# Attention of eight sampled queries rearranged inside a hybrid decoder layer, with the first layer norm applied later

## The chip, the cores and the metric

The kernel runs on one core of one Trainium2 chip. The metric is the device time of one execution in microseconds; lower is better. Engines are named as in the profile: PE (TensorE), PEld (its weight loads), DVE (VectorE), ACT (ScalarE), POOL (GpSimd) and SP (SyncE, which here only issues transfers).

## The reference

One decoder layer is applied to 1024 prompt positions and to 8 sampled tokens, each with 2048 cached positions. Cut to what matters here:

```python
def sparse_attend(q, ks, vs, valid):            # 8 heads of 64; 256 selected keys per query
    logits = einsum('bthd,btkhd->bthk', q, ks) * HEAD_DIM ** -0.5
    p = softmax(where(valid, logits, NEG_INF))
    return einsum('bthk,btkhd->bthd', p, vs)

def sample_attention(...):                      # per sampled token: indexer scores over 2048 + 1 keys
    _, idx = lax.top_k(sc, 256)
    ks = where(idx < past, cache_k[page, offset], k_new)      # rows of 512 floats, gathered
    vs = where(idx < past, cache_v[page, offset], v_new)
    return sparse_attend(q, ks, vs, valid)

def merge_and_channel_mix(x, attn, gm, ga, gb, ...):
    h = layer_norm(ALPHA * x + (ga * (attn @ w_a) + gb * (gm @ w_b)) @ w_o, ln1_g, ln1_b)
    f = hierarchical_moe(h, ...)                # top group of 4, then top 2 of its 8 experts
    return layer_norm(ALPHA * h + f, ln2_g, ln2_b)
```

The prompt attends in the same way over its own 1024 keys; there the kernel masks the keys that were not chosen instead of gathering the chosen ones.

## The kernel before

The program is a row of blocks. All engines leave a block together, and each engine runs its own instruction list in order; semaphores order the engines among themselves.

1. `project_and_score` makes q, k, v and the indexer scores.
2. `choose_keys_and_gate` finds the 256 best keys on DVE while PE makes the gates `gate_a` and `merged_b` (L787), which SP stores to DRAM (L710). At its end `keep["rows"]` holds the cache row numbers of the sampled queries.
3. `attend` is written out as 34 steps over `units`: 8 query tiles t = 7 down to 0, four head pairs each. In step s, PE makes the logits of unit s (L1173), transposes the probabilities of unit s-1 (`turn_probs`, L1187), and weighs the values for unit s-2 (`weigh`, L1200). DVE adds the masks and takes the minimum (L1385) and copies part of the transposed probabilities (L1296); ACT does the exponentials (L1312) and the other copies. After the last pair of a tile PE spreads the reciprocals of the sums (L1213), ACT copies them (L1323), and DVE scales the output (`share_out`, L1372). Tiles 7 to 4 have more than 512 keys and are called wide here, tiles 3 to 0 narrow. The eight sampled queries ride along: POOL issues their 48 indirect gathers (16 of cached K rows, 16 of cached V rows, 8 and 8 of own rows), each step's behind a chunk copy of that step (`wait_for_turn`). In steps 18 to 25, PE spreads query b over all 128 partitions (`spread_query`, L1222), and DVE multiplies and reduces both halves of its K rows (L1345, L1347). The maximum, exponential, normalisation, transposition and weighting of the sampled logits follow in steps 26 to 30; copying, turning and reading the sampled output (L1326, L1258, L1411) come after the loop.
4. `merge_route_and_experts` multiplies by `w_a` (L1639), merges with the gates, multiplies by `w_o` (L1668) for 9 token tiles, adds the residual (L1905), transposes, routes (`pick`), ranks (`place`) and scatters each token's place in a list to DRAM (L1607). DVE applies the first layer norm in two passes over a tile, subtract-and-gain (L1935) and scale-and-bias (L1943). SP stores the normalised tiles to `scratch["h"]` (L1590). POOL then gathers the tokens of the first packs from it (L1983). A pack is 128 rows; 24 packs pass through the class `Experts`: transpose rows (L2113), gate and up (L2100), transpose hidden (L2121), down (L2132), scatter (L2078). Copies L2145 (ACT) and L2184 (DVE) bring the transposed rows to SBUF. The first pack is put together on PE (`assemble_first`, L1730 and L1737). Expert weights come in with 2 MB (`w_gate_up`) and 1 MB (`w_down`) loads, four experts ahead. `Finish` makes the output with the second layer norm.

Of the kernel before, what the change touches and what calls it, by code (L numbers as in the profile page):

```python
# [20 lines left out]
P = 128  # L21
D = 1024
# [46 lines left out]
def project_and_score(nc, ins, outs, keep):  # L69
# [5 lines left out]
    with nc.cleanup_on_exit(), ExitStack() as ctx:  # L75
# [91 lines left out]
        def _(sp):  # L167
# [25 lines left out]
            sp.dma_start(outs["v_all"][SEQ:, :], zs[3 * FEW:3 * FEW + N_SAMPLE, :]).then_inc(few_out, 16)  # L193
            for t in range(NT):
# [20 lines left out]
            sp.wait_ge(few_out, 48)  # L215
# [172 lines left out]
        def _(act):  # L388
# [11 lines left out]
            def read(t, g):  # L400
                bank = FIRST_BANKS[g] if t == 0 else g % 2
                act.wait_ge(acc_full, 1 + 4 * t + g + 1)
                if g == 0 and t == 1:
                    act.wait_ge(few_out, 48)
                    act.wait_ge(turned_full, 1)
# [185 lines left out]

def choose_keys_and_gate(nc, ins, outs, keep, scratch):


    with nc.cleanup_on_exit(), ExitStack() as ctx:
# [85 lines left out]
        idle = [sem(f"idle{n}") for n in range(3)]  # L681

# [42 lines left out]
        def _(pe):  # L725
# [92 lines left out]
            make_gates(KC // 2 - 1, ahead=find_rows)  # L818

# [125 lines left out]
        def _(dve):  # L945
# [85 lines left out]
            step(nc.vector.tensor_copy(keep["rows"][:], rows_f[:]))  # L1031


def attend(nc, ins, outs, keep, scratch):
# [3 lines left out]
    PAIRS = HEADS // 2  # L1038
    n_qh = N_SAMPLE * HEADS
    with nc.cleanup_on_exit(), ExitStack() as ctx:  # L1040
# [9 lines left out]
        k_half = [keep["w_a"][:].rearrange("p a (b n) -> p (a b) n", n=AW), sb("k_sel", [P, N_SAMPLE, AW])[:]]  # L1050
        v_sel = sb("v_sel", [P, 2 * N_SAMPLE, AW])
        first = sb("first_masks", [P, 3 * P])
        probs = [sb(f"probs{j}", [P, 2, SEQ]) for j in range(2)]
# [7 lines left out]
        own_row = sb("own_row", [2, N_SAMPLE], U32)  # L1061
        lg = sb("lg", [P, 2, n_qh])
# [7 lines left out]
        k_in, v_in = sem("k_sel_in"), sem("v_sel_in")  # L1070
# [12 lines left out]
        q_spread = sem("q_spread")  # L1083
# [10 lines left out]
        query_at = {narrow + 2 + b: b for b in range(N_SAMPLE)}  # L1094
        MAX_AT, EXP_AT, PROBS_AT, TURN_AT, WEIGH_AT = (max(query_at) + n for n in (1, 2, 3, 4, 5))
# [4 lines left out]
        copies = [by[:i + 1].count(by[i]) for i in range(len(chunks))]  # L1100

# [18 lines left out]
        @block.sync  # L1120
        def _(sp):
            wait_for_gates_stored(sp)
            sp.dma_start(first[:], ins["first_masks"]).then_inc(const_in, 16)
            sp.dma_start(own_b[:], ins["rank"][:, 0:N_SAMPLE]).then_inc(own_in, 16)
            sp.wait_ge(lg_ready, N_SAMPLE // 2)
            sp.dma_start(keep["w_a"][:], ins["w_a"]).then_inc(w_a_in, 16)
            sp.wait_ge(w_a_in, 16)

        @block.gpsimd
        def _(pool):  # L1130
# [11 lines left out]
            def wait_for_turn(n):  # L1142
                wait_copied(pool, chunk_of[n, 1, units[n][0] // 4 * 4])

            for b in range(N_SAMPLE):
                wait_for_turn(b)
                for half in range(2):
                    gather(k_of, "cache_k", b, half, k_in)
            pool.wait_ge(own_ready, 1)
            pool.wait_ge(k_in, 32 * N_SAMPLE)  # L1150
            for b in range(N_SAMPLE):
                wait_for_turn(N_SAMPLE + b)
                gather_own(k_of, "k_all", b, k_in)
                gather(v_of, "cache_v", b, 0, v_in)
            pool.wait_ge(v_in, 16 * N_SAMPLE)
            for b in range(N_SAMPLE):
                wait_for_turn(2 * N_SAMPLE + b)
                gather(v_of, "cache_v", b, 1, v_in)
                gather_own(v_of, "v_all", b, v_in)
            pool.wait_ge(k_in, 48 * N_SAMPLE)  # L1160
            pool.wait_ge(v_in, 48 * N_SAMPLE)

        @block.tensor
        def _(pe):
            def make_logits(n):
                t, hp = units[n]
                if n >= 1:
                    pe.wait_ge(masked, 2 * n)
                width = (t + 1) * P
                for c in range(0, width, 512):  # L1170
                    c1 = min(width, c + 512)
                    for e in range(2):
                        mm = nc.tensor.matmul(ps[:, 2 * e + c // 512, 0:c1 - c],  # L1173
# [44 lines left out]
            def spread_query(b):  # L1218
                if b >= 2:
                    pe.wait_ge(lg_ready, b - 1)  # L1220
                for k in range(AW // P):
                    mm = nc.tensor.matmul(ps[:, 1 + 2 * (b % 2), k * P:(k + 1) * P],  # L1222
                                          qT[:, k, SEQ + b:SEQ + b + 1].to_broadcast([P, P]), ident[:],
                                          start=True, stop=True)
                mm.then_inc(q_spread, 1)

# [13 lines left out]
            def weigh_sample():  # L1240
                pe.wait_ge(pT_ready, 1)
                pe.wait_ge(v_in, 48 * N_SAMPLE)
# [9 lines left out]
            def turn_sample_out():  # L1252
                wait_copied(pe, len(chunks) - 2)
                wait_copied(pe, len(chunks) - 1)
                for g in range(2):
                    pe.wait_ge(s_copied, g + 1)
                    for k in range(AW // P):
                        mm = nc.tensor.transpose(ps[:, TURN + g, k * P:(k + 1) * P], product[g][:, k * P:(k + 1) * P], ident[:])  # L1258
                    mm.then_inc(s_turned, 1)

            for s in range(LAST):
                if s < N:
                    make_logits(s)
                if s in query_at:
                    spread_query(query_at[s])
# [4 lines left out]
                if s == WEIGH_AT:  # L1270
                    weigh_sample()
                if 0 <= s - 1 < N:
# [7 lines left out]
            turn_sample_out()  # L1280
# [19 lines left out]
        def _(act):  # L1300
            for s in range(LAST):
# [12 lines left out]
                if s == EXP_AT:  # L1314
                    act.wait_ge(lg_ready, N_SAMPLE + 2)
                    nc.scalar.activation(prob_s[:], ps[0:n_qh, 1, 0:TOPK], ACT.Exp, bias=stat_s[:, 1:2],
                                         scale=SCALE, accum_out=stat_s[:, 2:3]).then_inc(s_exped, 1)
                if s >= 2 and units[s - 2][1] == PAIRS - 1:
# [5 lines left out]
            for g in range(2):  # L1324
                act.wait_ge(s_out, g + 1)
                nc.scalar.copy(product[g][:], ps[:, 1 + 2 * g, :]).then_inc(s_copied, 1)  # L1326

        @block.vector
        def _(dve):
            step = Chain(dve, dve_step)  # L1330

            wait_for_gates_stored(dve)
# [1287 lines left out]
```

## Time and profile before

| | us |
|---|---|
| median of 3 runs | 1386.04 |
| lowest and highest | 1384.17, 1386.59 |
| the profiled execution, its own time | 1384.73 |
| its span, first to last instruction | 1383.1 |
| PE busy | 1320.8 (95%) |
| DVE busy | 717.7 (52%) |
| ACT busy | 280.1 (20%) |
| POOL busy | 241.0 (17%) |
| mean granted TensorE clock | 0.986 |

The profiled execution took 1.6 us more than its span. A matmul with fp32 operands appears as two entries, so counts of matmuls and weight loads are twice those in the source. Matmuls are pipelined: one entry's duration is longer than the distance to the next start, so in a dense stretch the distances are what counts. "Idle before" names what an engine waited for.

### The profile page before, as it was taken

The page shows a single profiled execution, that of the slowest core. Times are in us where ns is not written, and L with a number is a line of the kernel's source. Part 1 is how long each engine was busy: PE and PEld are TensorE (multiplying, and loading weights), DVE is VectorE, ACT ScalarE, POOL GpSimd, SP SyncE. Part 2 cuts the span into 40 slices and gives each one's busy share as a digit, 9 for nine tenths or more (in the row PEclk, how much of TensorE's full clock was granted, in tenths as well). Part 3 has the DMA queues.
Part 4 walks back from the last instruction along what each step waited for, and adds up shares of the span by engine and source line. Part 5 has one row for each costly group of instructions (what it writes and reads, how often), then busy time and mean ns, then how long its engine had stood idle before and what let it go on. Part 6 is the DMA issues. An engine that isn't in the chain of part 4 may idle for free. (4 is left out here: it accounts for less than half of the span.)

```text
span 1383.1 us, 19214 instructions
## 1 busy us (share of the span) xinstructions
PE 1320.8 (95%) x6689; PEld 679.1 (49%) x6689; DVE 717.7 (52%) x1709; ACT 280.1 (20%) x621; POOL 241.0 (17%) x292
## 2 busy tenths in 40 slices
PE   8999999899999999999899989999978999999994
PEld 2444444345466666666577656544443333333321
DVE  0211123589888988997265864588871111111135
ACT  0100112322221111111356430000001111111124
POOL 3222000043420000011133410011112111111113
PEclk9999999999999999999999999999999999999997
DMA  9311002210031111110032309831137999999936
GB/s 325 102 52 63 17 17 77 92 52 1 0 110 69 69 68 69 68 68 32 29 99 68 120 25 355 343 153 35 42 107 271 369 414 401 409 411 413 381 156 242
DMA packets 70316, 214.13 MB, mean 155 GB/s; under 512 B 16059, under 2 KB 41915, under 8 KB 59866
## 3 DMA queue, kind: packets, MB, share of 16 engines
q1 hardware_dynamic: 52810, 180.51, 34.7%
q0 software_dynamic: 12688, 27.76, 5.9%
q10 hardware_dynamic: 4736, 4.75, 1.1%
q8 instruction: 52, 0.85, 0.3%
q14 instruction: 30, 0.25, 0.1%
HBM read 186.47 MB, written 34.65 MB: 160 GB/s over the span
## 5 line engine op out<-in xcount | busy, mean ns | idle before, releaser
L262 PE MATMUL ps_mixer<-front,x_all 128*128 128x512 f32 (+1 forms) x448 | 180.4, 557 | 1.7 <-ACT wi L413 1.7
L959 DVE TENSOR_SCALAR_CACHE_REDUCE front<-score,bound 128x384 bf16<-128x384 f32 (+2 forms) x198 | 174.0, 940 | 0.4 <-DVE bound L981 0.3
L262 PEld LDWEIGHTS ps_mixer<-front,x_all 128*128 128x128 f32 x448 | 83.2, 190 | 91.7 <-issue 78.7
L1668 PE MATMUL ps<-w_o,mergedT 128*128 128x512 f32 x256 | 116.5, 601 | 0.0
L2100 PE MATMUL ps<-w_gate_up,w_o 128*32 128x512 f32 (+1 forms) x640 | 113.2, 594 | 1.7 <-DVE w_o L2184 1.7
L787 PE MATMUL ps_mixer<-x_all,front 128*128 128x344 f32 x384 | 114.4, 453 | 0.0
L787 PE MATMUL ps_mixer<-x_all,w_gate 128*128 128x344 f32 x384 | 113.3, 453 | 0.0
L2100 PE MATMUL ps<-w_a,w_o 128*64 128x512 f32 (+1 forms) x256 | 113.1, 595 | 0.0
L2209 DVE TENSOR_TENSOR w_o<-w_o,ps 128x256 f32<-128x256 f32 x24 | 10.1, 421 | 164.0 <-ACT w_o L2164 164.0
L787 PEld LDWEIGHTS ps_mixer<-x_all,w_gate 128*128 128x128 f32 x384 | 72.7, 190 | 37.5
L787 PEld LDWEIGHTS ps_mixer<-x_all,front 128*128 128x128 f32 x384 | 72.6, 190 | 37.1
L959 DVE TENSOR_SCALAR_CACHE_REDUCE front<-score_s,bound 8x2049 bf16<-8x2049 f32 x33 | 77.0, 2335 | 0.0
L1668 PEld LDWEIGHTS ps<-w_o,mergedT 128*128 128x128 f32 x256 | 46.0, 190 | 47.8 <-issue 47.8
L941 POOL TENSOR_TENSOR front<-front 128x344 f32<-128x344 f32 x24 | 25.2, 1050 | 243.7 <-ACT front L901 243.7
L2100 PEld LDWEIGHTS ps<-w_gate_up,w_o 128*32 128x32 f32 (+1 forms) x640 | 33.1, 115 | 69.0 <-issue 69.0
L2078 POOL DMA_INDIRECT pair_out<-w_o,entries x24 | 25.0, 1042 | 234.7 <-DVE w_o L2216 234.7
L898 ACT ACTIVATE front<-ps_mixer,gate_bias 128x344 f32<-128x344 f32 x48 | 26.2, 547 | 175.8 <-PE ps_mixer L787 175.7
L2132 PE MATMUL ps<-w_down,w_o 128*32 128x512 f32 (+1 forms) x320 | 59.3, 610 | 0.0
L2132 PE MATMUL ps<-gates,w_o 128*32 128x512 f32 (+1 forms) x128 | 58.1, 597 | 0.5 <-ACT w_o L2169 0.5
L735 PE MATMUL ps_mixer<-front,x_all 128*128 128x512 f32 x128 | 57.4, 592 | 0.0
L2100 PE MATMUL ps<-mergedT,w_o 128*32 128x512 f32 x384 | 56.5, 594 | 0.0
L1639 PE MATMUL ps<-attnT,w_a 128*128 128x344 f32 x186 | 54.0, 453 | 1.5 <-PEq L1040 1.5
(349 smaller groups left out, 1891.1 us busy)
## 6 DMA issues: line engine op xcount, KB each, us to landing
w_gate_up<-in_w_gate_up SPq DMA_DIRECT2D x16, 2048.0 KB, 14.4
w_down<-in_w_down SPq DMA_DIRECT2D x16, 1024.0 KB, 16.0
w_a<-in_w_gate_up SPq DMA_DIRECT2D x8, 2048.0 KB
mergedT<-in_w_gate_up SPq DMA_DIRECT2D x8, 2048.0 KB
gates<-in_w_down SPq DMA_DIRECT2D x8, 1024.0 KB, 7.1
mergedT<-in_w_down SPq DMA_DIRECT2D x8, 1024.0 KB
front<-in_w_qkvi SPq DMA_DIRECT2D x7, 930.0 KB, 18.0
w_gate<-in_w_gate SPq DMA_DIRECT2D x4, 1280.0 KB, 6.3
```

The costliest lines, as they stand in the source:

```text
L262: mm = nc.tensor.matmul(ps[:, g % 2, 0:c1 - c0], x_all[:, k, t * P:(t + 1) * P], w[:, k, c0:c1], start=(k == 0), stop=(k == KC - 1))
L735: mm = nc.tensor.matmul(ps[:, bank, :], x_all[:, k, t * P:(t + 1) * P], w_uv(k)[:, half * GW:(half + 1) * GW], start=(k == 0), stop=(k == ...
L787: mm = nc.tensor.matmul(ps[:, SETS[at % 2][which], 0:n], w_gate[j][:, which * KC + k, :], right[:, k, c0:c0 + n], start=(k == 0), stop=(k ...
L898: op = nc.scalar.activation(to, src, ACT.Sigmoid, bias=gate_bias[:, which, bass.ds(i * 2 + j, 1)])
L941: nc.gpsimd.tensor_tensor(m[:, 1, 0:n], m[:, 1, 0:n], m[:, 2, 0:n], ALU.mult).then_inc(multiplied, 1)
L959: V.tensor_scalar(waste[0:n, at - width:at], s, column(bound, g), None, compare, ALU.add, accum_out=column(number, g)).then_inc(taken, 1)
L1639: mm = nc.tensor.matmul(ps[:, FIRST_BANK + n % 3, 0:width], w_a[:, k, blk * P:(blk + 1) * P], attnT[:, k, c0:c0 + width], start=(k == 0), ...
L1668: mm = nc.tensor.matmul(ps[:, PROJECTED[i % 2][c], :], mergedT[:, k, t * P:(t + 1) * P], w_o[:, k, c * 512:(c + 1) * 512], start=(k == 0), ...
L2078: pool.indirect_dma_start(out=scratch["pair_out"].rearrange("t w q j d -> (t w q j) d"), out_offset=bass.IndirectOffsetOnAxis(ap=entries[: ...
L2100: mm = nc.tensor.matmul(ps[c0:c1, GU, :], rowsT[j][:, k, c0:c1], w_gu[b][:, k, :], start=(k == 0), stop=(k == KC - 1))
L2132: mm = nc.tensor.matmul(ps[c0:c1, 4 + 2 * j + c, :], hiddenT[j][:, k, c0:c1], w_dn[b][:, k, c * 512:(c + 1) * 512], start=(k == 0), stop=( ...
L2209: nc.vector.tensor_tensor(hidden[j], hidden[j], ps[:, GU, F:2 * F], ALU.mult).then_inc(hid, 1)
```

## The change

It has these parts.

- **Query rows by transfer.** The sampled q rows are stored to a scratch tensor in the first block; in `attend`, SP loads each of them to all 128 partitions (four buffers). `spread_query` goes, and the product reads both operands from SBUF.
- **Gathers.** `gather_all` issues them without waiting for chunk copies: two cache gathers of a sequence, then the own rows of the sequence before, each sequence on a semaphore of its own.
- **Half a query per step.** Steps 4 to 19 each take one half (128 keys) of a query's logits. The rest of the sampled chain moves to steps 21 to 27, its output's copy, turn and read among them (steps 26 and 27).
- **First logits.** PE makes unit 0's logits at the end of the gate block into PSUM banks that are free there; unit 1 has banks of its own, so that it waits for no mask. DVE does not wait for the gate stores at the start of `attend`, and prepares the own-row numbers after unit 0's masks.
- **Layer norm 1.** Only `z = (x - mean) * rstd` is made in the routing loop, in place, by ACT (one Identity activation per tile); `scratch["z"]` replaces `scratch["h"]`. Gain and bias are applied while the transposed rows are copied from PSUM: four activations on ACT and four tensor_scalar on DVE, of 128 x 128, instead of one copy of 128 x 512 each. DVE restores h in SBUF during the packs: `restore`, 18 passes of 128 x 1024.
- **Order in the routing tail.** SP loads the fourth `w_gate_up` after the last z stores and after the first gather has landed; POOL scatters the last tile's list before it gathers pack 1.

```diff
 choose_keys_and_gate, tensor:
             make_gates(KC // 2 - 1, ahead=find_rows)
+            pe.wait_ge(gates_read, 6 + (KC // 2 - 1) * 18 + 15)
+            pe.wait_ge(found_read, 1)
+            for c in range(2):
+                for e in range(2):
+                    mm = nc.tensor.matmul(ps[:, FIRST_LOGITS[e] + c, :], keep["qT"][...], keep["kT"][...], start=True, stop=True)
...
 attend:
-        query_at = {narrow + 2 + b: b for b in range(N_SAMPLE)}
-        MAX_AT, EXP_AT, PROBS_AT, TURN_AT, WEIGH_AT = (max(query_at) + n for n in (1, 2, 3, 4, 5))
+        query_at = {narrow - 2 * N_SAMPLE + 4 + n: (n // 2, n % 2) for n in range(2 * N_SAMPLE)}
+        MAX_AT, EXP_AT, PROBS_AT, TURN_AT, WEIGH_AT, COPY_AT, OUT_AT = (max(query_at) + 2 + n for n in range(7))
+        def bank_of(n, e):
+            return (FIRST_LOGITS, (0, OUT))[n][e] if n < 2 else 2 * e
...
+            for b in range(N_SAMPLE):
+                if b >= Q_AHEAD:
+                    sp.wait_ge(lg_ready, b - Q_AHEAD + 1)
+                sp.dma_start(q_rows[b % Q_AHEAD][:], scratch["q_few"][b:b + 1, :].to_broadcast([P, AW])
+                             ).then_inc(q_in[b % Q_AHEAD], 16)
...
+            def gather_all(to, cache, new, arrived):
+                for n in range(N_SAMPLE + 1):
+                    if n < N_SAMPLE:
+                        for half in range(2):
+                            gather(to, cache, n, half, arrived[n])
+                    if n >= 1:
+                        pool.wait_ge(own_ready, 1)
+                        pool.wait_ge(arrived[n - 1], 32)
+                        gather_own(to, new, n - 1, arrived[n - 1])
+            gather_all(k_of, "cache_k", "k_all", k_in)
+            gather_all(v_of, "cache_v", "v_all", v_in)
...
-                if n >= 1:
+                if n >= 2:
                     pe.wait_ge(masked, 2 * n)
...
 merge_route_and_experts, sync:
             for i, t in enumerate(tiles):
-                if i + 1 == TILES:
-                    sp.wait_ge(routed, TILES)
-                    sp.dma_start(keep["w_gate_up"][W_AHEAD][:], ins["w_gate_up"][W_AHEAD]).then_inc(keep["w_gu_in"][W_AHEAD], 16)
-                sp.wait_ge(h_ready, i + 1)
+                sp.wait_ge(scaled, i + 1)
...
+            sp.wait_ge(routed, TILES)
+            sp.wait_ge(keep["rows_in"][0], 16)
+            sp.dma_start(keep["w_gate_up"][W_AHEAD][:], ins["w_gate_up"][W_AHEAD]).then_inc(keep["w_gu_in"][W_AHEAD], 16)
...
 gpsimd:
-            pool.wait_ge(first_ready, 2)
-            pool.wait_ge(last_h_out, 32)
-            gather_rows(pool, scratch, keep["e_rows"][1], first_tokens[1], 0, keep["rows_in"][1])
             for which in range(2):
                 scatter(TILES - 1, which)
+            pool.wait_ge(first_ready, 2)
+            pool.wait_ge(last_z_out, 32)
+            gather_rows(pool, scratch, keep["e_rows"][1], first_tokens[1], 0, keep["rows_in"][1])
...
 scalar:
+                hb = h[:, tiles[t], :]
+                act.wait_ge(shifted, t + 1)
+                nc.scalar.activation(hb, hb, ACT.Identity, bias=shift[t % 2][:], scale=mv[t % 2][:, 1:2]).then_inc(scaled, 1)
...
 vector:
-                hb = h[:, tiles[i], :]
-                dve.wait_ge(h_turned, 2 * i + 2)
-                V.scalar_tensor_tensor(hb, hb, mean[:, 0:1], ln1[:, 0, :], ALU.subtract, ALU.mult).then_inc(gained, 1)
+                dve.wait_ge(powed, i + 1)
+                V.scalar_tensor_tensor(shift[i % 2][:], mean[:, 0:1], -1.0, mean[:, 1:2], ALU.mult, ALU.mult).then_inc(shifted, 1)
...
-                dve.wait_ge(gained, i + 1)
-                V.scalar_tensor_tensor(hb, hb, mean[:, 1:2], ln1[:, 1, :], ALU.mult, ALU.add).then_inc(h_ready, 1)
...
 Experts:
-            nc.scalar.copy(rowsT[j][:, 0:4, :], ps[:, 0, :].rearrange("p (k q) -> p k q", q=P)).then_inc(rowsT_act, 1)
+            for k in range(4):
+                gained = nc.scalar.activation(rowsT[j][:, k, :], ps[:, 0, k * P:(k + 1) * P], ACT.Identity,
+                                              bias=ln1_t[:, 1, k:k + 1], scale=ln1_t[:, 0, k:k + 1])
+            gained.then_inc(rowsT_act, 1)
...
+            def restore(e, jw):
+                t, which = e // 2, e % 2
+                if loaded and t < TILES:
+                    ...
+                    V.tensor_tensor(h[:, t, :], h[:, t, :], keep["ln1"][:, which, :],
+                                    ALU.add if which else ALU.mult).then_inc(restored, 1)
```

## Rows read from the trace of the kernel before

**Rows 1.** Stretches: busy time per engine, granted clock, DMA share and GB/s.

```profile
core 0: us, PE busy (x) PEld busy (x) DVE busy (x) ACT busy (x) POOL busy (x), PEclk, DMA share, GB/s
673.50:687.70 14.20, 9.29 (x35) 4.29 (x34) 5.92 (x13) 6.05 (x9) 0.00 (x0) 0.76 0.08 26
687.70:758.70 71.00, 71.00 (x719) 51.89 (x718) 41.73 (x89) 44.11 (x90) 26.49 (x28) 1.00 0.28 79
758.70:828.00 69.30, 59.84 (x550) 41.16 (x548) 50.27 (x147) 31.00 (x94) 19.08 (x21) 0.98 0.23 73
883.00:1009.00 126.00, 125.45 (x499) 60.93 (x497) 96.76 (x322) 10.82 (x24) 20.14 (x22) 1.00 0.31 113
1038.20:1064.60 26.40, 22.23 (x151) 8.65 (x151) 4.57 (x19) 4.51 (x9) 4.79 (x5) 0.94 0.76 287
1064.60:1332.00 267.40, 266.36 (x2009) 90.28 (x2008) 40.21 (x68) 42.73 (x89) 43.52 (x43) 1.00 0.92 371
```

**Rows 2.** Timeline at the start of attend: start, duration, operation, idle before.

```profile
675.73 3.52 PE L1173 MATMUL ps<-kT,qT 64*128 64x512 f32 x8 [2.20 <-PEq L595]
...
679.33 1.23 DVE L1385 CUSTOM_DVE_ANT_0 probs<-ps,score 128x1024 f32<-128x1024 f32 x1 [0.76 <-PE ps L1173]
...
681.77 2.75 PE L1173 MATMUL ps<-kT,qT 64*128 64x512 f32 x8 [2.52 <-DVE low L1385]
...
687.67 1.99 PE L1173 MATMUL ps<-kT,qT 64*128 64x512 f32 x8
```

**Rows 3.** Timeline of a step in the wide tiles that shares out.

```profile
751.63 0.69 DVE L1372 TENSOR_TENSOR attnT<-ps,shares 128x512 f32<-128x512 f32 x1
...
753.21 1.31 PE L1200 MATMUL ps<-probsT,early 128*64 128x128 f32 x20
```

**Rows 4.** Timeline of a narrow step: a query's two products and its spread.

```profile
771.38 0.68 DVE L1345 TENSOR_TENSOR product<-w_a,ps 128x512 f32<-128x512 f32 x1
...
772.58 0.97 PEld L1222 LDWEIGHTS ps<-ident,qT 128*128 128x128 f32 x8 [0.76 <-issue]
...
772.81 0.69 DVE L1345 TENSOR_TENSOR product<-w_a,ps 128x512 f32<-128x512 f32 x1
```

**Rows 5.** Timeline: logits of units 16 and 31, sampled values and output, next block.

```profile
758.75 1.13 PE L1173 MATMUL ps<-kT,qT 64*128 64x512 f32 x4
...
814.15 3.64 PE L1247 MATMUL ps<-v_sel,probT_s 128*32 128x512 f32 x32
...
818.46 0.49 PE L1173 MATMUL ps<-kT,qT 64*128 64x128 f32 x4
...
824.40 2.75 DVE L1411 COPY attnT<-ps 64x4 f32<-64x4 f32 x16 [0.50 <-PE ps L1258]
...
828.05 4.29 PE L1639 MATMUL ps<-attnT,w_a 128*128 128x344 f32 x14 [1.51 <-PEq L1040]
```

**Rows 6.** Timeline of the routing tail.

```profile
1021.15 1.01 POOL L1607 DMA_INDIRECT list_of<-entry,slot_out  x1 [0.19 <-issue]
...
1021.61 1.28 DVE L1935 SCALAR_TENSOR_TENSOR h_rows<-h_rows,mv,ln 128x1024 f32<-128x1024 f32 x1
...
1027.75 1.28 DVE L1943 SCALAR_TENSOR_TENSOR h_rows<-h_rows,mv,ln 128x1024 f32<-128x1024 f32 x1
...
1034.34 0.29 DVE L1872 TENSOR_TENSOR attnT<-attnT 128x128 f32<-128x128 f32 x1
...
1038.21 7.07 PE L2100 MATMUL ps<-w_gate_up,w_o 128*32 128x512 f32 x64 [1.34 <-DVE w_o L2184]
```

**Rows 7.** Chain that ended last, in time order: two gathers and the last scatter.

```profile
1023.78 7.59 DMA w_o<-h,first_tokens
...
1046.09 11.86 DMA w_o<-h,tokens
...
1332.79 3.62 DMA pair_out<-w_o,entries
```

**Rows 8.** Grouped instructions: ACT activations of 128 x 128; busy time, mean ns.

```profile
L871 ACT ACTIVATE front<-ps_mixer,b_sp 128x128 f32<-128x128 f32 x32 | 9.1, 363 | 6.6 <-PE ps_mixer L745 6.6
```

More of the change, by code:

```diff
@@ L1030, in _ @@
             step(nc.vector.scalar_tensor_tensor(rows_f[:], found[:, :, 0], float(P), found[:, :, 1], ALU.mult, ALU.add))
-            step(nc.vector.tensor_copy(keep["rows"][:], rows_f[:]))
+            nc.vector.tensor_copy(keep["rows"][:], rows_f[:]).then_inc(found_read, 1)
 def attend(nc, ins, outs, keep, scratch):
@@ L1038, in attend @@
     PAIRS = HEADS // 2
+    Q_AHEAD = 4
     n_qh = N_SAMPLE * HEADS
@@ L1061, in attend @@
         own_row = sb("own_row", [2, N_SAMPLE], U32)
+        q_rows = [sb(f"q_rows{j}", [P, AW]) for j in range(Q_AHEAD)]
         lg = sb("lg", [P, 2, n_qh])
@@ L1082, in attend @@
         dve_step = sem("a_dve_step")
-        q_spread = sem("q_spread")
+        q_in = [sem(f"q_rows_in{j}") for j in range(Q_AHEAD)]
         lg_ready = sem("lg_ready")
@@ L1141, in _ @@
             wait_for_gates_stored(pool)
-            def wait_for_turn(n):
-                wait_copied(pool, chunk_of[n, 1, units[n][0] // 4 * 4])
-            for b in range(N_SAMPLE):
[L1146 to L1161, printed above, removed]
+            def gather_all(to, cache, new, arrived):
[9 more added lines that the diff above has]
+            gather_all(v_of, "cache_v", "v_all", v_in)
+            for b in range(N_SAMPLE):
+                pool.wait_ge(k_in[b], 48)
+                pool.wait_ge(v_in[b], 48)
         @block.tensor
@@ L1317, in _ @@
                                          scale=SCALE, accum_out=stat_s[:, 2:3]).then_inc(s_exped, 1)
+                if s == COPY_AT:
+                    for g in range(2):
+                        act.wait_ge(s_out, g + 1)
+                        nc.scalar.copy(product[g][:], ps[:, 1 + 2 * g, :]).then_inc(s_copied, 1)
                 if s >= 2 and units[s - 2][1] == PAIRS - 1:
@@ L1466, in merge_route_and_experts @@
         mv = [sb(f"mv{j}", [P, 2]) for j in range(2)]
+        shift = [sb(f"shift{j}", [P, 1]) for j in range(2)]
         places = over[:, 2 * D + 6 * P:2 * D + 8 * P]
@@ L2454, in _ @@
             last.vector_spread(dve)
-            dve.wait_ge(h_in, 32 * TILES)
+            dve.wait_ge(h_in, 32 * (TILES + 1))
+            for t in range(TILES):
+                for which, op in enumerate((ALU.mult, ALU.add)):
+                    nc.vector.tensor_tensor(h[:, t, :], h[:, t, :], ln1[which], op).then_inc(restored, 1)
+                    dve.wait_ge(restored, 2 * t + which + 1)
             last.vector(dve)
```

175 lines of the change are left out of this document (96 added, 79 removed).

## Prediction

> **What bounds the kernel now.** I read the page's slices first, then the windows cut at the places where the blocks and the kinds of step change, then the timeline inside the windows in which PE is not full, and last the chain of waits. [Rows 1] is the result. In three stretches PE has no idle time worth naming: the wide tiles of attend (71.00 of 71.00), the routing loop (125.45 of 126.00) and the packs (266.36 of 267.40). There, work moved between DVE, ACT, POOL and DMA is free until it holds PE up. Three other stretches leak: the start of attend (PE busy 9.29 of 14.20, clock 0.76), the narrow tiles (59.84 of 69.30) and the routing tail with the first packs (22.23 of 26.40 after 1038.20, clock 0.94). The change touches all six, so it is worth what it returns in the last three less what it costs in the first three. In the timeline of attend's start the reader is to see a serial chain: PE idle 2.20, eight slow matmuls of 3.52, two masks, and logits of unit 1 that wait 2.52 for them [rows 2]. In the tail it is a chain of transfers: a first gather of 7.59 and a later one of 11.86 [rows 7], each of which PE needs.
>
> **Part 1, first logits: -5.5.** Before, unit 2's logits start at 687.67 [rows 2]. After, unit 0's logits follow the last gate matmul at once. PE ended at 675.73 - 2.20 = 673.53, and eight such matmuls at full clock take 1.99 [rows 2], so they end near 675.5. A block begins about 1 us after its predecessor's last work (2.20 of idle held 0.7 of SP's last store issues, which the logits now cover, and the rest is the border; 1.51 at the next border [rows 5]). So attend begins near 676.5. DVE has its scores ready and starts the two masks at once, 2 x 1.23, to 678.9; the two of unit 1, whose logits no longer wait, come after the own-row numbers (their transfer lands about 0.5 behind the first masks), to about 681.9. Unit 2's logits need these and start at about 682.2. That is 5.5 earlier. Bounds: -7 if nothing stands between the mask pairs; -4 if the border is 2.20 long and the clock stays low behind it. The small own-row steps on DVE are hidden in the wait for the transfer.
>
> **Part 2, half a query per wide step: +1.6.** Steps 4 to 15 get one product and reduction of 128 x 512 each, 12 of the 16 halves. One half costs DVE 772.81 - 771.38 = 1.43 [rows 4]. DVE has room: it is busy 41.73 of 71.00, and 12 x 1.43 = 17.2 make it 58.9 [rows 1]. The price is one of place, not of sum. In an ordinary step what DVE delays is a mask, due only in the next step. Where a tile is shared out, the scaling ends at 751.63 + 0.69 = 752.32 and PE starts the weighing that overwrites its bank at 753.21 [rows 3]: 0.89 of slack against 1.43 of new work, 0.54 late. Three such steps (tiles 7, 6 and 5) fall where a half rides: 3 x 0.54 = 1.6. Bounds: 0 if the share-out stays ahead of the half product, +4 if also the last wide tile's short steps each lose some tenths.
>
> At this place the Trainium skill, "SBUF — State Buffer", section "SBUF: two separate sides", speaks against the change: a DVE operation with two SBUF inputs and a GpSimd operation that reads SBUF take a shared pair of ports one after the other, for a whole instruction. The trace points the other way: a DVE pass with two SBUF inputs took 1.28 (1021.61 to 1022.89) though POOL's indirect scatter ran from 1021.15 to 1022.16 beside it, the same 1.28 as the pass at 1027.75 [rows 6]. By the row this costs nothing; its own result is a rival below.
>
> **Part 3, narrow tiles to the next block: -8.9.** Units 16 to 31 start at 758.75 and 818.46, the next block's matmul at 828.05 [rows 1, 5]. Removed from PE are 8 spreads, 0.97 of weight loads each with the start of the next behind it, about 1.0: -8.0 [rows 4]. Removed from DVE are 16 halves, of which four come back in steps 16 to 19: 12 x 1.43 = 17.2 off 50.27 [rows 1]. PE's 9.46 of idle does not go with it: in narrow tiles a step is shorter than the chain logits, mask, exponential, transposition, copy, and ACT's 31.00 stay. I take 1.2 of it as going. The sampled weighing of 3.64 [rows 5] only moves to an earlier step. At the end the sampled output's turn and the 2.75 of small copies [rows 5] are ahead of the last units, and the last unit's own chain takes their place: -0.6. Somewhere near that chain a pause of PE may bring the clock down, as at 0.76 after the pause in [rows 1, 2]: +0.9. Sum -8.0 - 1.2 - 0.6 + 0.9 = -8.9. Bounds: -5 (the spreads had only filled time in which PE would have waited anyway, three of the eight come back as idle) and -14 (nearly half of the 9.46 goes too).
>
> **Part 4, routing tail: -7.5.** In the loop ACT gains one 128 x 1024 pass per tile and has the room, 10.82 of 126.00; DVE loses two passes of 1.28 per tile and gains a tiny one. PE is full there, so both are free [rows 1, 6]. In the tail DVE is on the path. The last tile's first pass of 1.28 stood ahead of the token list for the first gather, so that gather issues about 0.8 earlier than 1023.78 [rows 6, 7]. It took 7.59 beside the fourth 2 MB load, which now comes later; a transfer of as many rows with little beside it took 3.62 [rows 7], and I take 4.7, nearer to that, since the stores of the last tiles are still beside it. It lands at 1023.0 + 4.7 = 1027.7 instead of 1031.37, 3.7 earlier. Before, the first pack's L2100 came 1038.21 - 1031.37 = 6.84 behind the landing [rows 6, 7]; after, the two copies are four pieces each. A piece of 128 x 128 costs DVE about 0.29 [rows 6] and ACT 0.36 [rows 8], so 1.2 to 1.5 where one copy of 128 x 512 stood (about 0.7): +0.5. But DVE's final 1.28 [rows 6] is gone from ahead of the placing, which bounded the other operand: another -0.4. L2100 starts at about 1034.6: -3.6. From there to the third pack's L2100 it took 26.4, in which PE was busy 22.23 [rows 1]. The 11.86 of the gather at 1046.09 [rows 7] ended it. This gather waits on lists that also come 3.6 earlier and on SP's and POOL's queues, in which the loads that stand beside it come later. Without it the stretch is PE's work, 22.2 less the slow clock (6% of 22.2 is 1.3), plus 1.4 of other short waits and the pieces: 22.3. That is -4.1 more, and with a rounding of 0.2, -7.5. Bounds: -2 (the gathers stay as slow as 11.86 and 7.59, only the DVE pass is gained) and -8.5 (3.62 each).
>
> **At no cost.** The q rows (8 transfers of 256 KB on SP, in stretches with a DMA share of 0.23 to 0.28), the extra store in the first block, and 18 restoring passes of about 1.28 in the packs (23 us on a DVE busy 40.21 of 267.40) [rows 1, 6]. The four pieces per copy in the packs are covered by PE's other matmuls of a pack; without that cover they cost 24 x 0.5 = 12, but a PE with 1.04 idle in 267.40 shows how early its inputs are. The gathers no longer pace themselves: POOL's 49 operations in attend took 45.57, 0.93 each [rows 1], so a sequence of three takes 2.8, and 6.4 if every one also waits a landing of 3.62 [rows 7]. DVE wants a new sequence's rows every second step, some 9 us.
>
> **Sum.** -5.5 + 1.6 - 8.9 - 7.5 = -20.3. The profiled execution's own time is 1384.73 (span 1383.1), so 1364.4; the median shown is 1.3 above that execution: 1365.7, say **1366**.
>
> **Rivals.** (A) The forecast, 0.59, own range 1361 to 1371. (B) The fourth 2 MB load, moved behind the first gather, meets the second pack's gather instead and stretches it as 11.86 was; the tail gives -2: 1371. For it: DMA share 0.76 in that stretch [rows 1]. Chance 0.15. (C) The gate block now ends with PE, and the border and a low clock keep most of the start's gain; -5.5 becomes -2.5: 1369. Chance 0.09. (D) Narrow tiles lose 5 more of their idle: 1360 to 1361. Chance 0.05. (E) The half products stand on the path in all 12 wide steps: +17 for +1.6, 1381. Against it: 29 us of idle DVE in 71. Chance 0.04, a quarter of it less than 0.2% from before. (F) DVE's 16 half products each wait behind POOL's gathers: up to 11 meet one, 0.93 each, 1376. Its rule is that of the Trainium skill named above; against it stands the row of 1.28. Chance 0.03. (G) Slower: gathers come too late. DVE takes its list in order, so that a product that waits for its K rows holds masks and copies behind it and with them PE. From 676.5 on POOL has until unit 19 for the K gathers, about 86 us, 10.8 for each sequence; to lose all 20.3 each would need 10.8 + 20.3 / 8 = 13.3, twice the 6.4 above. At the 11.86 of the worst gather it costs 8 x 1.1 = 8.5, which leaves a gain; the case begins at 13.3 and gives 1386 and up. Chance 0.05, of which 0.03 slower by over 0.2%, 0.02 within.
>
> **Range and chances.** 0.2% (2.8 us) is about what a measurement of this kernel can tell from no change. The likeliest case gives 1366. The range 1358 to 1376 takes in A to D and F with the bounds of their terms, and leaves out E, G and tails of the rest, under 2 in 10. Faster 0.94 (A, B, C, D, F, most of E and nothing of G), within 0.2% 0.03, slower 0.03.
>
> **What would show it.** Part 1: unit 2's logits at about 682. Part 2: unit 16 at about 755, no wait of PE for DVE over 1 us between. Part 3: the first L1639 at about 815, PE idle still near 8 in the narrow tiles. Part 4: a first gather of 5 us or less, the first pack's L2100 about 16 and the third pack's about 20 earlier than before. After that the packs still take 12 each and the end follows; a longer distance from the third pack's L2100 to the end would show that the pieces, the restoring passes or DMA hold the packs. Wrong would be a PE that waits in wide steps for DVE with K rows behind it, or a second gather of 10 us.

## The result, and the profile after

| | us |
|---|---|
| changed kernel, median of 4 runs | 1415.7 (1414.65 to 1417.01) |
| kernel before, beside it | 1385.11 (1381.61 to 1386.59) |
| ratio, with its 95% interval | 1.023 (1.0217 to 1.0242) |
| the changed kernel's profiled execution, own time | 1414.65 (span 1413.0) |

The forecast was 1366 with a range of 1358 to 1376. The kernel became 30 us slower. The same code took 1362.6 and 1362.8 in two later groups of runs and 1417.8 and 1420.2 in two others, each group on one chip; that is the subject of the experiments.

The page's slices after (35.3 us each) show at a glance where the time stands.

```profile
PE   8999999899999999999647998999997999999985
...
PEclk9999999999999999999957999999999999999998
```

PE is at 6 and 4 tenths in slices 20 and 21, and its clock is down. The windows, cut at 4 us inside that place, say it more sharply; the columns are those of [rows 1].

```profile
core 0: us, PE busy (x) PEld busy (x) DVE busy (x) ACT busy (x) POOL busy (x), PEclk, DMA share, GB/s
...
692.00:696.00 4.00, 4.00 (x44) 3.01 (x43) 1.60 (x4) 3.21 (x6) 2.78 (x3) 1.00 0.49 149
696.00:700.00 4.00, 2.10 (x7) 0.75 (x6) 0.00 (x0) 0.00 (x0) 3.07 (x4) 0.95 0.47 130
700.00:704.00 4.00, 0.00 (x0) 0.00 (x0) 0.00 (x0) 0.00 (x0) 3.08 (x4) 0.50 0.48 137
...
740.00:744.00 4.00, 1.49 (x2) 0.37 (x2) 0.00 (x0) 0.00 (x0) 3.06 (x4) 0.50 0.49 149
...
748.00:752.00 4.00, 0.59 (x3) 0.62 (x4) 1.43 (x3) 0.00 (x0) 0.00 (x0) 0.50 0.00 0
752.00:756.00 4.00, 4.00 (x33) 3.67 (x33) 3.25 (x6) 2.82 (x5) 0.00 (x0) 0.50 0.02 4
...
696.00:752.00 56.00, 19.54 (x66) 9.62 (x66) 5.13 (x10) 3.23 (x6) 35.88 (x38) 0.56 0.42 118
```

Between 696 and 752 PE is busy 19.54 of 56 us, DVE 5.13 and ACT 3.23, at times none of them for 4 us, while POOL works on for some 3 of every 4 us until its gathers end. This stretch is called the hole below. The DMA share is 0.42, so the transfer engines are not full. The low clock comes after the standing and is not its cause: from 696 to 700 PE was already down to 2.10 of 4.00 at a clock of 0.95. The timeline of the same place shows what kind of standing it is (start, duration, operation, idle before).

```profile
688.16 0.95 POOL L1160 DMA_INDIRECT w_a<-out_k_all,own_row  x1 [4.77 <-issue]
...
693.51 0.08 DVE L1406 DVE_READ_ACCUMULATOR2_ANT low<- 128x1 f32 x1
694.04 1.09 PE L1205 MATMUL ps<-ident,probs 128*128 128x128 f32 x8
...
710.15 0.69 DVE L1303 COPY probsT<-ps 128x512 f32<-128x512 f32 x1 [16.55 <-DMA early<-in_kidx_pool]
...
732.06 1.20 PE L1191 MATMUL ps<-kT,qT 64*128 64x512 f32 x1 [0.40 <-issue]
733.48 1.01 PE L1191 MATMUL ps<-kT,qT 64*128 64x512 f32 x1 [0.21 <-issue]
734.88 1.01 PE L1191 MATMUL ps<-kT,qT 64*128 64x512 f32 x1 [0.39 <-issue]
...
747.06 0.93 POOL L1160 DMA_INDIRECT v_sel<-out_v_all,own_row  x1 [2.36 <-DMA v_sel<-in_cache_v,rows]
...
750.57 1.29 DVE L1303 COPY probsT<-ps 128x512 f32<-128x512 f32 x2 [31.44 <-DMA early<-in_kidx_pool]
751.77 0.68 DVE L1351 TENSOR_TENSOR product<-w_a,q_rows 128x512 f32<-128x512 f32 x1
```

Two signs matter. PE's logits matmuls at 732 to 735 wait for nothing that the profile shows and yet start 1.4 apart, where eight entries took 1.99 in [rows 2], and 3.52 at the low clock. And DVE starts a copy at 710.15 whose input PE had turned by 695.13, 15 us before. The transfer that the row names as releaser is one of an earlier block, so it can't be the cause. The first half product comes only at 751.77. So no product, and no wait of DVE for K rows, lies ahead of the hole. It begins some 8 us into POOL's second run of gathers (from 688.16) and ends about 3 us behind the last of the 48, at 747.06 + 0.93.

### The profile page after: what moved, and what is told of

The parts are those of the page before. It is cut to its first block and busy times, and to the rows that moved or that the text cites. A ratio compares the mean times of both kernels' runs of the same rounds, so it can differ in the third digit from the quotient of the medians.

```text
span 1413.0 us, 19279 instructions
## 1 busy us (share of the span) xinstructions
PE 1322.3 (94%) x6625; PEld 677.1 (48%) x6625; DVE 736.9 (52%) x1790; ACT 313.0 (22%) x702; POOL 246.5 (17%) x292
## 5 line engine op out<-in xcount | busy, mean ns | idle before, releaser
L263 PE MATMUL ps<-front,x_all 128*128 128x512 f32 (+1 forms) x448 | 180.4, 557 | 1.7 <-ACT wi L414 1.7
L263 PEld LDWEIGHTS ps<-front,x_all 128*128 128x128 f32 x448 | 83.2, 190 | 91.7 <-issue 78.7
L792 PE MATMUL ps<-x_all,front 128*128 128x344 f32 x384 | 114.4, 453 | 0.0
L792 PE MATMUL ps<-x_all,w_gate 128*128 128x344 f32 x384 | 113.3, 453 | 0.0
L792 PEld LDWEIGHTS ps<-x_all,w_gate 128*128 128x128 f32 x384 | 72.7, 190 | 37.5
L792 PEld LDWEIGHTS ps<-x_all,front 128*128 128x128 f32 x384 | 72.6, 190 | 37.1
L1205 PE MATMUL ps<-ident,probs 128*128 128x128 f32 x288 | 46.7, 295 | 28.1 <-DVE probsT L1303 23.5
L954 POOL TENSOR_TENSOR front<-front 128x344 f32<-128x344 f32 x24 | 28.6, 1192 | 241.6 <-ACT front L914 241.6
L911 ACT ACTIVATE front<-ps,gate_bias 128x344 f32<-128x344 f32 x48 | 26.2, 547 | 177.1 <-PE ps L792 177.0
L1303 DVE COPY probsT<-ps 128x512 f32<-128x512 f32 (+3 forms) x48 | 22.1, 485 | 70.2 <-DMA early<-in_kidx_pool 52.3
L740 PE MATMUL ps<-front,x_all 128*128 128x512 f32 x128 | 57.4, 592 | 0.0
```

Source lines behind the costliest of these rows:

```text
L263: mm = nc.tensor.matmul(ps[:, g % 2, 0:c1 - c0], x_all[:, k, t * P:(t + 1) * P], w[:, k, c0:c1], start=(k == 0), stop=(k == KC - 1))
L740: mm = nc.tensor.matmul(ps[:, bank, :], x_all[:, k, t * P:(t + 1) * P], w_uv(k)[:, half * GW:(half + 1) * GW], start=(k == 0), stop=(k == ...
L792: mm = nc.tensor.matmul(ps[:, SETS[at % 2][which], 0:n], w_gate[j][:, which * KC + k, :], right[:, k, c0:c0 + n], start=(k == 0), stop=(k ...
L954: nc.gpsimd.tensor_tensor(m[:, 1, 0:n], m[:, 1, 0:n], m[:, 2, 0:n], ALU.mult).then_inc(multiplied, 1)
L1205: mm = nc.tensor.transpose(ps[:, TURN + i % 2, k * P:(k + 1) * P], probs[n % 2][:, e, (c + k) * P:(c + k + 1) * P], ident[:])
```

## Where the 30 us stand

The stages as the prediction cut them, from the starts of the same matmuls. (The prediction rounded its last two, -3.6 and -4.1, to -7.5 in its sum.) "Later chip" is the changed kernel again on a chip without the hole (g0_after, own time 1364.48).

| stage | before | forecast | changed, result | changed, later chip |
|---|---|---|---|---|
| last gate matmul's end to unit 2's logits | 14.14 | -5.5 | 8.58 (-5.6) | 8.57 (-5.6) |
| to unit 16's logits | 71.08 | +1.6 | 123.53 (**+52.5**) | 71.58 (+0.5) |
| to the next block's first matmul | 69.30 | -8.9 | 57.55 (-11.8) | 58.76 (-10.5) |
| to the first pack's gate and up | 210.16 | -3.6 | 208.30 (-1.9) | 208.40 (-1.8) |
| to the third pack's | 26.4 | -4.1 | 21.75 (-4.6) | 21.74 (-4.6) |

The rows of the result (each the first of its stage), and then those of the later chip:

```profile
683.34 1.99 PE L1191 MATMUL ps<-kT,qT 64*128 64x512 f32 x8
...
806.87 1.13 PE L1191 MATMUL ps<-kT,qT 64*128 64x512 f32 x4
...
864.42 1.97 PE L1658 MATMUL ps<-attnT,w_a 128*128 128x344 f32 x6 [1.03 <-PEq L1054]
...
1072.72 7.07 PE L2121 MATMUL ps<-w_gate_up,w_o 128*32 128x512 f32 x64 [2.02 <-DVE w_o L2210]
...
1094.47 0.62 PE L2121 MATMUL ps<-w_a,w_o 128*32 128x512 f32 x1
```

```profile
683.58 1.99 PE L1191 MATMUL ps<-kT,qT 64*128 64x512 f32 x8
...
755.16 1.13 PE L1191 MATMUL ps<-kT,qT 64*128 64x512 f32 x4
...
813.92 54.02 PE L1658 MATMUL ps<-attnT,w_a 128*128 128x344 f32 x186 [1.03 <-PEq L1054]
...
1022.32 7.07 PE L2121 MATMUL ps<-w_gate_up,w_o 128*32 128x512 f32 x64 [2.02 <-DVE w_o L2210]
...
1044.06 0.62 PE L2121 MATMUL ps<-w_a,w_o 128*32 128x512 f32 x1
```

The five stages of the result sum to +28.6. The blocks ahead of them ended 1.2 later in this execution, together 29.8 of the 29.9 that are 1414.65 - 1384.73. Four of the five stages came out as gains. The whole loss is one stage.

## The experiments

Six groups were run. Each ran on one chip, with the kernel before beside its members; the chip is given by its number.

| group | chip | kernel | us | kernel before | ratio (95%) |
|---|---|---|---|---|---|
| 1 | 5 | e1_paced | 1362.89 | 1382.31 | 0.9862 (0.9841 to 0.9883) |
| | | e2_before_unpaced | 1383.17 | | 1.0002 (0.999 to 1.0014) |
| | | e3_products_later | 1364.63 | | 0.9881 (0.9848 to 0.9913) |
| 2 | 3 | e4_after_again | 1362.62 | 1382.44 | 0.9858 (0.983 to 0.9887) |
| | | e5_one_step_later | 1365.32 | | 0.9885 (0.9852 to 0.9918) |
| | | e6_v_after_unit9 | 1365.69 | | 0.9873 (0.9835 to 0.9911) |
| 3 | 4 | e7_after_third | 1420.15 | 1384.66 | 1.0264 (1.0238 to 1.0291) |
| | | e8_logits_inside | 1419.43 | | 1.0262 (1.0243 to 1.028) |
| | | e9_load_ahead | 1419.79 | | 1.0268 (1.0246 to 1.0291) |
| 4 | 4 | f0_after | 1417.8 | 1383.88 | 1.0244 (1.0222 to 1.0266) |
| | | f1_paced | 1381.09 | | 0.9972 (0.9959 to 0.9984) |
| | | f2_before_unpaced | 1426.56 | | 1.0308 (1.029 to 1.0327) |
| | | f3_v_after_unit9 | 1407.22 | | 1.0167 (1.0149 to 1.0186) |
| 5 | 12 | g0_after | 1362.78 | 1381.95 | 0.9857 (0.9825 to 0.989) |
| | | g1_two_per_step | 1371.46 | | 0.9923 (0.99 to 0.9946) |
| | | g2_plain | 1366.14 | | 0.9882 (0.9847 to 0.9916) |
| 6 | 8 | h1_two_per_step | 1374.15 | 1382.88 | 0.9937 (0.9912 to 0.9962) |
| | | h2_plain | 1365.45 | | 0.9872 (0.9846 to 0.9899) |

**Group 1: the burst, or the products?** The theory was that the unbroken run of gathers slows the engines; the rivals were the products and the query rows. e1_paced puts the waits back into the changed kernel's gathers:

```diff
                 for n in range(N_SAMPLE + 1):
+                    wait_copied(pool, chunk_of[at + n, 1, units[at + n][0] // 4 * 4])
                     if n < N_SAMPLE:
```

> The changed kernel with one edit: each sequence's gathers (two of the cache, one of own rows of the sequence before) wait for the last chunk copy of the step's unit again, K in steps 0 to 8, V in steps 9 to 17. Theory A (the unbroken run of gathers itself slows TensorE's stream and delays its signals; this costs the 50 us between 696 and 752): the wide tiles return to about 71 us, unit 16's logits start near 755, and the time is 1361 to 1370. Theory B (the half products stand behind K rows that come late, or their two SBUF inputs collide with POOL): the products stay where they are, K rows come even later than now, so at most a few us come back, 1400 to 1420. Theory C (the query rows' transfers to all partitions do it): unchanged, about 1415.

e2_before_unpaced takes them out of the kernel before:

```diff
             for b in range(N_SAMPLE):
-                wait_for_turn(b)
...
-                wait_for_turn(N_SAMPLE + b)
...
-                wait_for_turn(2 * N_SAMPLE + b)
```

> The kernel before with one edit: its 48 gathers no longer wait for chunk copies (16 of K, then own rows and V as before, back to back); everything else as before: queries spread by PE, products in narrow steps. Theory A: the wide tiles lose some 40 to 50 us, time 1425 to 1440. Theories B and C, and any that needs the new products, the q transfers or the first logits: 1383 to 1390, no change.

e3_products_later moves the sampled chain:

```diff
-        query_at = {narrow - 2 * N_SAMPLE + 4 + n: (n // 2, n % 2) for n in range(2 * N_SAMPLE)}
+        query_at = {narrow - 2 * N_SAMPLE + 9 + n: (n // 2, n % 2) for n in range(2 * N_SAMPLE)}
```

> The changed kernel with its half products and the rest of the sampled chain five steps later (steps 9 to 24, maximum at 26, output at 31 and 32). No product lies within the first nine steps, in which the gathers run. Theory A: the loss stays, the first nine steps are as slow as now, time 1412 to 1422. Theory B: the loss in the wide tiles goes, 1365 to 1380.

The answers contradicted each other. e1 hit theory A's number, 1362.9. But e2 lost nothing (1.0002), which denies A, and e3 lost the hole too, which by its own terms spoke for the products. e3 and the changed kernel are the same program on every engine up to the first product, and the hole stands ahead of that product. So the program could not be the difference, and the next group had the changed kernel itself in it, unaltered beside the edited ones. Such a run is called the control of its group.

**Group 2: the same code again.** e4_after_again is the changed kernel unaltered.

> The changed kernel once more, unaltered, beside the kernel before. Theory D (the loss belongs to this program: something in its order of steps 3 and 4 and its run of gathers): 1412 to 1418, with the same hole between 696 and 750. Theory E (the loss belongs to where and when it ran, and not to the code): about 1363, as the two variants before.

> The changed kernel with the sampled chain one step later (half products in steps 5 to 20); gathers unchanged. Theory D with the first product's wait for its K rows and query row as the trigger: the hole shrinks or goes as that wait comes one unit (5.8 us) later, 1362 to 1400. Theory D with the gathers as the trigger: 1412 to 1418. Theory E: about 1363, the same as the changed kernel beside it.

e6 adds one wait: `wait_copied(pool, chunk_of[9, 1, 4])` ahead of the V gathers.

> The changed kernel, but the V gathers begin only behind unit 9's chunk copies; the K gathers stay back to back. Theory D: the part of the hole that lies beside the V gathers (716 to 748, some 30 us of 50) goes, 1380 to 1390. Theory E: about 1363.

All three came to 1363 to 1366: theory E. e1's hit in group 1 had shown nothing, since there was no hole on that chip to remove. The edits of e5 and e6 made about 3 us at most, and their runs overlap those of the control.

**Group 3: a third load, and two parts undone.** e8_logits_inside makes unit 0's logits at the start of attend again; e9_load_ahead puts the fourth gate-and-up load back ahead of the last tile's stores.

> The changed kernel unaltered, loaded a third time. Two loads of the same code gave 1415.7 and 1362.6 us. If the hole belongs to the chip or the load, this falls on one of the two: 1361 to 1369, or 1412 to 1418 with the hole between 696 and 750 again. Theory F (a hole of varying size, by chance of timing in the run of gathers): something between.

> The changed kernel with unit 0's logits made at the start of attend again, in the same banks as now; unit 1 still waits for no mask and DVE not for the gate stores. Part 1's sum: 3.5 at the low clock stand in attend again, unit 2's logits near 685 to 686, 2 to 3.5 slower than the changed kernel, 1365 to 1367 where that is 1363. Rival C of the prediction: no difference.

> The changed kernel with the fourth gate-and-up load ahead of the last tile's stores again, as in the kernel before. By part 4 of the prediction the first gather gets slow (7 us or more instead of 4 to 6) and 3 to 4 us are lost: 1366 to 1367 where the changed kernel has 1363. By rival B the load only changes which gather it meets: no difference within 1.5.

All three had the hole. Neither undone part has to do with it. What each part is worth can't be read from the times, for the hole varies by more than the 2 to 4 us in question: 1419.4 and 1419.8 beside 1420.2. The traces show it, since both parts lie outside the hole. In e8 the last gate matmul ended 2.21 ahead of the first of these rows, and unit 2's logits are the second:

```profile
679.02 2.60 PE L1263 MATMUL ps<-kT,qT 64*128 64x512 f32 x8 [2.21 <-PEq L599]
...
687.21 1.99 PE L1183 MATMUL ps<-kT,qT 64*128 64x512 f32 x8
```

That is 10.40 where the changed kernel has 8.58, so unit 0's logits under the gate block are worth 1.8 of part 1's 5.6, a little under the 2 to 3.5 expected. In e9 the first gather is slow, as expected:

```profile
1058.10 9.47 DMA w_o<-z,first_tokens
```

It took 6.29 in the result and 6.25 in f0_after below. The stage to the first pack's gate and up took 211.52, against 208.52 to 208.89 in e7, e8 and f0_after. Up to the third pack's it took 233.3, against 230.3 to 231.2. So in these traces, one execution each, moving the fourth load is worth some 2 to 3 us, and rival B's "no difference within 1.5" doesn't hold.

**Group 4: cause and cure on one chip.** The chip is the one of group 3, again with a control.

> The changed kernel unaltered, as the control of this group. It is the measure of the chip: about 1363 on a chip that does not show the hole, about 1416 to 1420 on one that does.

> The changed kernel with its gathers paced by the steps' chunk copies (as in the first group). Theory A (POOL's unbroken run of gathers is what slows the three other engines, on a chip that shows it): where the control has 1418, this has 1361 to 1368 and no hole. Theory G (anything else of the change does it on such a chip, the query rows' transfers, products from SBUF, z): 1410 or more.

> The kernel before with its 48 gathers unpaced (as in the first group). Theory A: where the control has the hole, this has one too, 1410 to 1435. Theory G: 1381 to 1387, as before.

> The changed kernel with the V gathers behind unit 9's chunk copies. Theory A: where the control has the hole, this has it beside each of its two runs of gathers; the same 48 gathers slow the engines for as long in all, so 1400 to 1420. Theory H (the run must be long, some 6 gathers with no gap, and costs more the longer it is): between, 1385 to 1405.

The control had the hole. Taking the waits out of the kernel before, with nothing else of the change in it, cost 1426.56 - 1383.88 = 42.7 us. Putting them into the changed kernel took 1417.8 - 1381.09 = 36.7 off it. The same window of four kernels, the busy times of PE, DVE and POOL being the first, third and fifth: f0_after,

```profile
688.00:752.00 64.00, 18.16 (x103) 11.14 (x100) 7.15 (x13) 6.67 (x12) 39.15 (x42) 0.58 0.41 114
```

f2_before_unpaced,

```profile
688.00:752.00 64.00, 34.63 (x184) 20.44 (x180) 12.40 (x21) 11.28 (x22) 36.84 (x39) 0.65 0.36 102
```

f1_paced,

```profile
688.00:752.00 64.00, 61.03 (x618) 44.47 (x618) 48.07 (x97) 36.65 (x74) 29.01 (x29) 1.00 0.43 133
```

and e2_before_unpaced, the same code as f2, from chip 5.

```profile
688.00:752.00 64.00, 64.00 (x648) 46.77 (x648) 37.67 (x79) 40.00 (x79) 37.89 (x40) 1.00 0.37 106
```

POOL issues as many gathers in f2 as in e2, 39 and 40 in 64 us. PE's entries fall from 648 to 184. So on chip 4 the run of gathers is enough to hold up the other engines, with nothing else of the change in the program, and on chip 5 it costs nothing. Theory A was right on the cause, but its 1361 to 1368 for f1_paced was missed by 13 us: this pacing is only part of the cure.

The price grows with how close the gathers stand. In f1_paced they come three to a step in the wide tiles, and PE is busy 40.69 of 42.00; in the narrow steps seven and six stand back to back (POOL's starts from 752.82 to 760.31 and from 768.89 to 775.34), and PE has 37.48 of 45.00 and the clock falls. The last row is e1_paced, the same code on chip 5.

```profile
688.00:730.00 42.00, 40.69 (x406) 29.12 (x404) 29.78 (x57) 23.58 (x46) 20.82 (x21) 1.00 0.36 104
730.00:775.00 45.00, 37.48 (x354) 27.17 (x352) 30.36 (x70) 22.11 (x49) 22.69 (x23) 0.92 0.46 143
...
730.00:775.00 45.00, 44.74 (x458) 32.25 (x458) 39.60 (x96) 29.89 (x68) 24.54 (x25) 1.00 0.49 153
```

From unit 2's to unit 16's logits f1_paced took 74.5 and e1_paced 71.6; from there to the next block 70.1 and 57.8. So on chip 4 the gathers three to a step cost 2.9 us, and those of the narrow steps 12.3.

f3_v_after_unit9, with two groups of 24, has two holes, one beside each (PE 27.04 of 42.00, and 13.19 of 25.00).

```profile
688.00:730.00 42.00, 27.04 (x200) 18.14 (x198) 15.19 (x27) 10.79 (x20) 16.38 (x18) 0.72 0.26 75
...
775.00:800.00 25.00, 13.19 (x84) 8.80 (x86) 9.81 (x24) 6.62 (x15) 10.98 (x12) 0.66 0.30 84
```

Its 1407 lies in the range that "the same gathers slow the engines as long" was given (1400 to 1420), 11 below the control. Theory H's 1385 to 1405 was missed by 2, so this run alone doesn't part the two.

**Groups 5 and 6: is spacing the cure, and does it take the indirect kind?**

> The changed kernel unaltered, as the control that tells which kind of chip it is: 1361 to 1369 or 1414 to 1421.

> The changed kernel with its 48 gathers in the same order, two to a step in steps 0 to 23, each pair behind the step's last chunk copy, so that POOL pauses after every pair. On a chip that shows the hole, theory A with a price that grows with the length of a run: 1362 to 1372 (three to a step had 1381 there, with its loss in the narrow steps). If only the number of gathers counted and not their spacing: 1381 or more. On a chip without the hole: 1361 to 1368.

> The changed kernel with each of its 48 gathers replaced by an ordinary transfer of as many rows, issued by POOL at the same places: it leaves out the choice of the rows, so the sampled outputs are not the reference's. On a chip that shows the hole: if any unbroken run of transfers issued by POOL does it, 1410 or more; if it takes the indirect kind, 1361 to 1372.

The chip had no hole, so neither question got an answer. g1 was 8.7 slower than its control all the same: with two gathers to a step the last V rows come late, and PE waits for them in front of the sampled weighing.

```profile
787.43 5.36 PE L1265 MATMUL ps<-v_sel,probT_s 128*32 128x512 f32 x32 [5.46 <-DMA v_sel<-out_v_all,own_row]
```

Both kernels were run once more:

> The changed kernel with two gathers to a step, again. On the chip without the hole it took 1371.5. On one with it, theory A with a price that grows with the length of a run: 1366 to 1376, the same as there within a few us, and below the 1381 of three to a step; if only the number of gathers counts: 1385 or more.

> The changed kernel with ordinary transfers by POOL in the place of its gathers, again (it leaves out the choice of the rows). On the chip without the hole it took 1366. On one with it: if any unbroken run of transfers issued by POOL does it, 1410 or more; if it takes the indirect kind, 1361 to 1372.

This was a fifth chip, and there was no control on it. In the same 64 us PE was busy 63.70 in h1 and h2, as in g0: no hole, and both questions stay open. h2's 1365.45 and g2's 1366.14 beside 1362.78 say only that ordinary transfers in the place of the gathers gain nothing where there is no hole.

## Why the prediction was wrong

**The failed step** is part 2 and, with it, the sentence "The gathers no longer pace themselves", which stood under "At no cost". The prediction weighed POOL's run of gathers for whether the rows come in time (rival G, 1386 and up) and for a shared port with DVE's products (rival F, 1376). It never asked what the run does to engines that have nothing to do with the gathers. In [rows 1] the kernel before shows POOL busy 26.49 of 71.00 beside a PE without idle. That is 28 gathers in pairs with gaps; a run of 24 back to back is in no row of before, and an unknown was costed at nothing without a bound. On the chip of the result this term was +52.5 where the text had +1.6. It missed by 50.9, and the median missed 1366 by 49.7: the step is the whole error.

**Rival G** had the right sign, but its mechanism was not what happened: at 751.77 DVE went straight from a copy into the first product, with no wait for K rows between them. It was held up before it ever came to one.

**The other steps held.** On a chip without the hole the changed kernel took 1362.6 and 1362.8, inside the own range of the forecast's case. The gain on the kernel before beside it was 19.8 and 19.2, where the sum had 20.3. That agreement is partly luck, as errors cancel (the figures without the hole are those of the later chip in the table):

- Part 1, -5.5: measured -5.6 twice. Unit 0's logits under the gate block and unit 1's banks did what was worked out; rival C didn't occur. Of the 5.6, 1.8 are the former (e8).
- Part 2, +1.6: +0.5 without the hole. Less than the 3 x 0.54 taken for the late share-outs.
- Part 3, -8.9: -10.5 and -11.8. The mis-sized term is PE's idle in the narrow tiles: it fell from 9.46 to 5.46 and 5.77, by some 4 where 1.2 was taken, and the "idle still near 8" of the prediction was missed.
- Part 4, -3.6 to the first pack: -1.8. The mis-sized term is the first gather, which took 6.32 where 4.7 was taken (before: 7.59), as the next row shows. SP now issues the last tile's two stores at 1008.46, right beside it; before, they came at 1029.07, 5.3 us into the gather. That they hold it up was not tested. From its landing to the first pack's gate and up it took 7.58, 0.7 more than before, where 0.1 more was taken. The fourth load's move did work (e9).
- Part 4, -4.1 to the third pack: -4.6. The slow gather of 11.86 is off PE's path there. It is not always: in e7 and f1 a gather of 11.73 and 12.63 stood on the chain that ended last, and the stage took 22.66 and 23.46 instead of 21.7 to 21.8. Rival B's tail of -2 in all didn't occur.
- The packs: from the third pack's gate and up to the last block's first matmul 277.13 before, 277.34 on the later chip. The restoring passes and the four pieces cost nothing, as costed.

```profile
1008.42 6.32 DMA w_o<-z,first_tokens
```

Rival F's rule found no support: on chips without the hole the products cost the wide tiles 0.5 in all, with POOL issuing beside them.

**What stays open.** Why chip 4 (in both of its groups) and the chip of the result show the hole, and chips 3, 5, 8 and 12 do not, was not found. The chip of the result has no number here; it may be chip 4, and that it is of that kind rests on its trace having the same hole. With one numbered chip that shows the hole, that it belongs to the chip, and not to something else that differed between the groups, is likely but not shown. Nor was it found what the engines lack. In the Trainium skill, "Runtime: NRT & Kernel Launch", section "Instruction fetch mechanics", each engine gets its instructions in blocks by DMA while it runs; a queue that starves behind gathers would fit engines that creep with nothing to wait for. Between 690 and 750 the trace has one packet of the instruction queue q8, and g0_after, without the hole, has five (packets, MB, share of the 16 engines; the changed kernel's result, then g0_after):

```profile
q8 instruction: 1, 0.02, 0.1%
```

```profile
q8 instruction: 5, 0.08, 0.6%
```

But an engine that runs few instructions also asks for few blocks, so the count fits a slow engine as well as a starved one. In these 60 us PE and PEld ran 232 entries in the result and 1214 in g0_after, some 240 to a packet in both. And a block that feeds so many would give long standing and then bursts, while much of the hole is PE creeping by single entries 1.4 apart. This is a conjecture, not a finding. Late signals between the engines would explain DVE's 15 us, but not PE's 1.4 between matmuls that wait for none. No version keeps the whole gain on both kinds of chip: the paced kernel took 1362.9 (e1) on a chip without the hole and 1381.1 (f1), still a ratio of 0.9972, on one with it. That is the best of what was run on both.

## What to carry to other kernels

A wait that only paces a queue may be what protects the others from it. Before it is dropped, look in the trace for a run as long and as dense as the one it would allow, and if there is none, bound the cost, for every engine and not only for those that use the data. And when an experiment's answers contradict each other, run the unaltered kernel beside them first: a cause is shown only where the control has the effect.

## What was not expected of the hardware

- On chip 4 (and on the chip of the result) 48 indirect gathers issued by POOL, most of them 1.25 us apart, bring PE, DVE and ACT nearly to a stop: in 64 us PE ran 103 entries instead of 646, at a DMA share of 0.41, for 55 us in all (f0_after beside g0_after: 1417.8 and 1362.8). The Trainium skill, "SBUF — State Buffer", section "SBUF: two separate sides", has PE and ACT wait for no other engine's port; that is no help here, as PE and ACT were held up without a wait that the profile names.
- The hole starts late. In the result four gathers in a row (678.48 to 683.39) did nothing, and PE fell to single entries some 8 us after the next run began; this took about 7 us in e7 and f0 and 15.7 in f2. It ended 0.6 to 4 us behind the last gather of a run. The kernel before has its gathers in pairs every 3 to 6 us, with one run of four, and lost nothing like it on the same chip (1383.9 there, 1382.3 on chip 5).
- Chips can differ much for one program and hardly for another: the medians of the kernel before lie within 0.2% of each other (1381.95 to 1384.66) on chips that part the changed kernel by 4%.
